# An even mixer in which the turned probabilities, not the scores, have two places in PSUM

## What is computed

```python
q, k, v, u, vv = split(z @ w_in)              # z: normed tokens; the context rows go through the same w_in
q, k = rms_norm(q) , rms_norm(k)              # per head, then rope on the 512 tokens
s = q @ k.T * dh ** -0.5                      # keys: a window of 1 to 3 blocks of 128, and the 256 context tokens
p = softmax(concat([s, sink]))[..., :-1]      # 8 heads, 6 query tiles of 128: 48 units
a = p @ v
u, vv = gelu(u), gelu(vv)
b = u * (ws @ rms_norm(vv) + bias)            # mixing inside chunks of 128 tokens, 8 groups
y = concat([a, b]) @ w_out
```

## Time and profile before

| | us |
|---|---|
| median of three runs | 3274.41 (3272.14 to 3275.29) |
| the profiled execution | 3274.63 |
| its span, first to last instruction | 3272.8 |
| PE busy | 3183.9 (97%) |
| DVE busy | 2219.2 (68%) |
| ACT busy | 1233.5 (38%) |

### The profile page before, as it was taken

The page is one execution under the profiler, slowest core; times in us unless marked ns, Lnnn a source line. Parts: engine busy times, 40 slices in busy tenths (PEclk is TensorE's granted clock), DMA queues, the critical chain, the costliest instruction groups (busy, mean ns, idle before and its releaser), DMA issues.

```text
span 3272.8 us, 50687 instructions
## 1 busy us (share of the span) xinstructions
PE 3183.9 (97%) x20376; PEld 2930.7 (90%) x20376; DVE 2219.2 (68%) x3792; ACT 1233.5 (38%) x2091; POOL 86.4 (3%) x189
## 2 busy tenths in 40 slices
PE   8999999998999999989999999989999999999999
PEld 6999999988899999989999999878888878788877
DVE  4979896466587777777777777675333666566754
ACT  4111112357553343354433343563222432334432
POOL 0000000001100000010000001000000000000100
PEclk9999999999999999999999999999999999999999
DMA  5545553210222222231222222112223321122232
GB/s 223 187 168 188 176 182 129 86 34 27 53 85 67 90 77 92 84 94 59 78 84 92 102 65 97 54 49 96 98 91 102 125 84 34 62 82 71 73 103 97
DMA packets 95321, 314.17 MB, mean 96 GB/s; under 512 B 11424, under 2 KB 15712, under 8 KB 93552
## 3 DMA queue, kind: packets, MB, share of 16 engines
q1 hardware_dynamic: 88128, 290.04, 26.4%
q0 software_dynamic: 6960, 20.88, 2.3%
HBM read 300.39 MB, written 4.19 MB: 93 GB/s over the span
## 4 chain that ended last, share of the span: by engine, by line
PE 48%; DVE 4%; ACT 2%; issue 1%; DMA 0%; ACTq 0%; DVEq 0%; SPq 0%
PE psum L690 32%; PE psum L1167 9%; DVE rawl L669 1%; PE psum L2842 1%; PE psum L1904 1%; DVE h L774 1%; PE psum L1887 1%; ACT wh L659 0%; PE psum L2865 0%; PE psum L2851 0%; PE psum L1728 0%; PE psum L3771 0%; DMA raw<-in_wdn 0%; PE psum L3289 0%; PE psum L1895 0%
## 5 line engine op out<-in xcount | busy, mean ns | idle before, releaser
L690 PE MATMUL psum<-zh,wh 128*128 128x512 f32 (+4 forms) x2352 | 756.6, 367 | 17.0 <-DVE ev L752 7.5
L659 ACT ACTIVATE wh<-raw 128x512 fp32r<-128x512 f32 (+3 forms) x551 | 447.3, 818 | 862.0 <-PE psum L690 471.5
L690 PE MATMUL psum<-zh,rawl 128*128 128x512 f32 (+4 forms) x2352 | 735.6, 358 | 0.0
L690 PE MATMUL psum<-zl,wh 128*128 128x512 f32 (+4 forms) x2340 | 732.2, 358 | 0.0
L669 DVE TENSOR_TENSOR rawl<-raw,wh 128x512 fp32r<-128x512 f32 (+3 forms) x551 | 502.6, 927 | 241.7 <-ACT wh L659 240.5
L690 PEld LDWEIGHTS psum<-zh,wh 128*128 128x128 f32 x2352 | 430.3, 189 | 69.3 <-issue 26.5
L1167 PE MATMUL psum<-formq,wh 128*128 128x386 f32 x1848 | 479.4, 341 | 10.2 <-DVE formq L971 3.5
L690 PEld LDWEIGHTS psum<-zh,rawl 128*128 128x128 f32 x2352 | 433.2, 189 | 41.2
L690 PEld LDWEIGHTS psum<-zl,wh 128*128 128x128 f32 x2340 | 431.0, 189 | 39.6 <-issue 2.9
L1167 PEld LDWEIGHTS psum<-formq,wh 128*128 128x128 f32 x1848 | 337.6, 189 | 15.3 <-DVE rawl L669 4.8
L774 DVE SCALAR_TENSOR_TENSOR h<-psum,mod,h 128x512 f32<-128x512 f32 (+1 forms) x288 | 169.9, 627 | 185.8 <-PE psum L690 185.6
(11 more groups left out here) (497 smaller groups left out, 4534.5 us busy)
## 6 DMA issues: line engine op xcount, KB each, us to landing
raw<-in_wup SPq DMA_DIRECT2D x176, 512.0 KB, 4.1
modw<-in_mod_w SPq DMA_DIRECT2D x128, 512.0 KB, 3.6
raw<-in_w_sw SPq DMA_DIRECT2D x36, 512.0 KB, 3.5
raw<-in_wdn SPq DMA_DIRECT2D x64, 256.0 KB, 3.7
raw<-in_wdn SPq DMA_DIRECT2D x32, 448.0 KB, 3.4
adaw<-in_ada_w SPq DMA_DIRECT2D x8, 1024.0 KB, 16.1
raw<-in_wdn SPq DMA_DIRECT2D x16, 512.0 KB, 3.9
raw<-in_od_in SPq DMA_DIRECT2D x16, 512.0 KB, 3.4
```

The lines of the kernel that those rows point to most:

```text
L659: nc.scalar.activation(hi_of(n, i), x, ACT.Copy).then_inc(w_hi, 1)
L690: last = nc.tensor.matmul(psum[:, at + to:at + to + e - s], w[:, q * P:(q + 1) * P], x[:, q, s:e], start=(q == 0 and j == 0), stop=(q == s ...
```

## The change

- From unit 32 on the turned probabilities have two places in turn (`turned_at`: E_PT, or column 0 for even units), and the scores keep their one. So every score now waits for the maximum of the unit just before, and the transposes from unit 33 on wait for the copy of the second unit before. Unit 32's transposes wait for the last uv drain, which its scores did before.
- From turn 33 on PE does the transposes ahead of the values.
- Mixing steps 0 to 5 go to turns 24 to 29, steps 6 to 11 to turns 34, 36, 38, 39, 41 and 43. `mb`, the buffer of the mixing on DVE, moves to a place of its own beside `ev_pt`, since in turns 24 to 29 the gate's buffer, whose place it shared, is in use.
- On DVE the drain of a uv tile comes right behind the maximum, ahead of division, inverse and all that follows. The lower keys of the second group go to turn 2. GELU of gate row 0 and the square behind it go from the last turn ahead of the units to turn 0.
- The order of the finished rows' split changes with the mixing.

```diff
-        mb = sb("mb", R_AT + words(2, T), [2, P])
+        mb = sb("mb", SCR_AT + words(4, 640), [2, P])
...
-                self.own_s = 1024 if u < SECOND_S or u % 2 else 0
+                self.turned_at = E_PT if u < SECOND_S or u % 2 else 0
...
-                return psum[:, self.own_s + c:self.own_s + c + w]
+                return psum[:, E_S + c:E_S + c + w]
...
-        DRAIN, CUBE, TANH, GELU = at(-3, 0), at(-2, 1), at(-2, 2), at(-1, 3)
-        VV_SQUARE, VV_GAIN, VV_SUM = [{i: k for i, k in x.items() if k < 4} for x in (at(-1, 3), at(0, 4), at(1, 5))]
+        DRAIN, CUBE, TANH, GELU = at(-3, 0), at(-2, 1), at(-2, 2), at(0, 3)
+        VV_SQUARE, VV_GAIN, VV_SUM = [{i: k for i, k in x.items() if k < 4} for x in (at(0, 3), at(0, 4), at(1, 5))]
...
-        MIX_STEPS = {34 + s: s for s in range(12)}
-        CAT_ROWS = [QROW, QROW + 1, QROW + 2, UROW, UROW + 1, UROW + 2, UROW + 3, QROW + 3]
-        CAT_CHUNKS = [4, 5, 6, 0, 1, 2, 3, 7]
-        CAT_STEPS = {31: 0, 33: 1, 39: 2, 42: 3, 44: 4, 47: 5, 48: 6}
+        MIX_STEPS = {24 + s: s for s in range(6)} | {34: 6, 36: 7, 38: 8, 39: 9, 41: 10, 43: 11}
+        CAT_ROWS = [QROW, QROW + 1, UROW, UROW + 1, QROW + 2, UROW + 2, UROW + 3, QROW + 3]
+        CAT_CHUNKS = [4, 5, 0, 1, 6, 2, 3, 7]
+        CAT_STEPS = {31: 0, 33: 1, 35: 2, 37: 3, 40: 4, 45: 5, 47: 6}
...
-                if i == SECOND_S:
-                    pe.wait_ge(drained, all_drained(EU))
-                elif i:
-                    pe.wait_ge(scores_read, i if i < SECOND_S else i - 1)
+                if i:
+                    pe.wait_ge(scores_read, i)
...
-                if i >= 1:
-                    pe.wait_ge(at_pc, i)
+                if i == SECOND_S:
+                    pe.wait_ge(drained, all_drained(EU))
+                elif i >= 1:
+                    pe.wait_ge(at_pc, i if i < SECOND_S else i - 1)
                 for j in range(len(u.vals)):
-                    last = nc.tensor.transpose(psum[:, E_PT + j * P:E_PT + (j + 1) * P],
+                    last = nc.tensor.transpose(psum[:, u.turned_at + j * P:u.turned_at + (j + 1) * P],
...
                 if i in VV_STEPS:
                     vv_rows_pe(pe, VV_STEPS[i])
+                if i in MIX_STEPS:
+                    mix_pe(pe, MIX_STEPS[i])
...
+                if i <= NE:
+                    transposes(i - 1)
                 if i % 2:
                     values(i - 3)
-                if i <= NE:
-                    transposes(i - 1)
...
+            def drain_beside(i):
+
+                if i in DRAIN:
+                    drain_row(dve, EU, EU.n[DRAIN[i]], ev[:, VVROW + DRAIN[i]])
...
+                drain_beside(turn - EV_TURNS)
                 beside_dve(dve, run, turn - EV_TURNS, 3)
-                if turn >= 3:
-                    g = turn - 3
-                    dve.wait_ge(ek_hi, EK_HI + g + 1)
-                    nc.vector.tensor_tensor(kl[:, g, :], ev[:, KROW + g, :], kh[:, g, :], ALU.subtract).then_inc(ek_lo, 1)
+                if turn == 3:
+                    keys_lower(0)
...
                 if 1 <= i < NE:
                     maximum(i)
+                drain_beside(i)
+                if i == 2:
+                    keys_lower(1)
```

More of the change, by code:

```diff
@@ L2210, in beside_dve @@
             row = lambda k: ev[:, VVROW + k, :]
-            if i in DRAIN:
-                k = DRAIN[i]
-                drain_row(dve, EU, EU.n[k], ev[:, VVROW + k])
             if i in GELU:
@@ L2441, in even_act @@
                         act.wait_ge(at_pv, (i - 1) // 2 * 2)
-                    nc.scalar.activation(ev_pt[:, u.u % 2, 0:u.w], psum[:, E_PT:E_PT + u.w], ACT.Copy).then_inc(at_pc, 1)
+                    nc.scalar.activation(ev_pt[:, u.u % 2, 0:u.w], psum[:, u.turned_at:u.turned_at + u.w],
+                                         ACT.Copy).then_inc(at_pc, 1)
                 if i >= 3 and i % 2:
@@ L2478, in maximum, with keys_lower @@
                                         ALU.mult, ALU.min).then_inc(at_s, 1)
+            def keys_lower(g):
+                dve.wait_ge(ek_hi, EK_HI + g + 1)
+                nc.vector.tensor_tensor(kl[:, g, :], ev[:, KROW + g, :], kh[:, g, :], ALU.subtract).then_inc(ek_lo, 1)
+            def drain_beside(i):
+                if i in DRAIN:
+                    drain_row(dve, EU, EU.n[DRAIN[i]], ev[:, VVROW + DRAIN[i]])
             run = Along(EU)
```

## The result

The changed kernel takes **3286.74 us** (median of five runs, 3285.95 to 3289.67). The kernel before, run beside it, takes 3275.18 (3272.14 to 3275.7). The ratio is 1.0039, with a 95% interval of 1.0029 to 1.0050: slower, by 0.4%. The forecast of +6.8 us had the direction and about half of the size. The measured time lies 0.7 us above the range.

A forecast was written before the change was run, and what follows sets the result against it. TensorE was taken as the bound nearly everywhere, with no hole until unit 30 and waits after. Terms -2.9 + 3.5 + 7.6 - 1.4 = +6.8 on 3274.63 gave 3281.4 us, range 3273 to 3286.

The forecast's parts named there:

- Term 1: Units 0 to 2: second uv tile's drain goes ahead, two short stalls, clock stays up; -2.9 us, bounds -4.3 and -1.3.
- the bound of one shorter spell (-1.3): Start, units 0 to 2: the clock falls once more, 3.2 us of work at half, 1.6 lost; sum -1.3 us.
- Term 2: Unit 20: PE waits 3.0 us for turned gate rows copied behind the drain, clock falls; +3.5 us, bounds +1.9 and +4.5.
- Term 3: Units 24 to 29: six mixing steps of 0.59 us plus waits at units 25, 26, 28; +7.6 us, bounds +6 and +9.
- Term 4: From unit 30: double turned probabilities, single scores, fewer mixing steps; lag 1.6, pairs -3.0; -1.4 us, bounds +1.6 and -7.9.
- The lag: Unit 30: last drain stands ahead of division, inverse and mixing, so unit 31's maximum and what follows come later; +1.6 us.
- The pairs: Five pairs of units, maximum of unit 36 to that of 46: 25.7 us in place of 28.73; -3.0 us.
- The end after unit 46 stays: Stretch behind unit 46's maximum: claimed to keep its length, no change.
- The tail did not pay back: Rival, tail: PE runs at its own work from unit 36, term 4 at -7.9; 3274.9 us, no change; chance 0.32.
- the 5.8 above which the prediction called itself wrong: Sign for the tail: pairs over 5.8 us, or under 4.6 us, would show the forecast wrong.
- Not all waits went: Faster rival, from unit 30: all PE waits go, term 4 at -16.4, sum -8.2; 3266.4 us; chance 0.06.
- The clock did not swing in units 20 to 29: Rival, units 20 to 29: stalls bring one longer low spell, 2.6 us more, sum +9.4; 3284.0 us; chance 0.12.

The follow-up runs named there:

- e7_late_division: Changed kernel with DVE dividing a pair's sums one turn later, behind the next maximum, from unit 34 on; 3285.98 us, ratio 1.0032.
- e5_square_early: Kernel before with only the second uv tile's drain ahead, lower keys at unit 2 and gate row 0's GELU product one turn earlier; 3270.27 us, ratio 0.9982.
- e1_drains_back: Changed kernel with the drains of units 1 and later back behind divisions, turned gate rows' copy and mixing's DVE part; 3280.43 us, ratio 1.0022.
- e9_mix_covered: Changed kernel with the first six mixing steps at odd units 23 to 33 in place of 24 to 29; 3283.99 us, ratio 1.0032.
- e4_places_back: Changed kernel with two places for scores and one for turned probabilities again, as before; 3282.31 us, ratio 1.0028.
- e3_values_first: Changed kernel with values ahead of transposes on PE again from unit 31 on; 3289.29 us, ratio 1.0051.
- e2_mix_back: Changed kernel with all twelve mixing steps in units 34 to 45 and the casts' order of before; 3278.72 us, ratio 1.0012.
- e6_order: Kernel of e5_square_early with transposes ahead of values from turn 33 on, two score places; 3268.51 us, ratio 0.9983.

## Why the prediction was wrong in size

- **Term 1: -2.9 forecast, -0.41 measured.** Both stalls came as worked out (1.3 and 1.4 forecast, 1.32 and 0.99 measured). The step that failed is "the nearest row is 803.5 to 807.4, idle 2.73 of 3.9 us, and there the clock stayed at 1.00. So I let it stay." The clock fell and stayed low over 6.8 us, also beyond the bound of one shorter spell (-1.3). In the forecast's own terms, -1.7 - 2.6 + 1.4 came out as -1.73 + 0.33 + 0.99: the 2.6 us of lower clock did not go. That the clock is the cause is shown from two sides: where nearly the same stalls did not bring it down (the execution of e7_late_division) the start was -2.75, close to the -2.9; and with one stall taken away (e5_square_early) the spell was 3.4 us long and the start -2.54. The one row in which it had held was not evidence enough, since it was one execution. And another row of the same trace spoke against it. The low spell at 847.4, which the earlier trace rows has, came behind three waits of PE that were all shorter than 1.3 us:

```profile
844.10 0.66 PE L2363 MATMUL psum<-ev_pt,vdup 128*64 128x128 f32 x8 [0.88 <-ACT ev_pt L2442]
...
846.16 0.41 PE L2350 MATMUL psum<-ident,ev_s 128*128 128x128 f32 x2 [0.82 <-ACT ev_pt L2442]
847.33 1.12 PE L2363 MATMUL psum<-ev_pt,vdup 128*64 128x128 f32 x8 [0.76 <-ACT ev_pt L2442]
```

- **Term 2: +3.5 forecast, +3.36 measured.** Right in place, in mechanism (the copy of the turned gate rows behind the drain) and in the choice that the clock falls. e1_drains_back takes it back whole. Its lower bound, +1.9 with no fall, is close to what e7_late_division's execution shows (+1.74).
- **Term 3: +7.6 forecast, +8.45 measured.** The waits came at the three units named, 1.59, 1.15 and 1.04 us (1.5, 1.3 and 1.3 forecast). The term mis-sized is the step itself: 0.59 was taken from mixing row to score row, but 8.45 less the three waits, 3.78, leaves 0.78 for each of the six, and the four steps without waits of e9_mix_covered cost 0.72. The clock stayed at 1.00 in these units, as forecast.
- **Term 4: -1.4 forecast, +1.8 measured** (+1.14, -0.93, +1.58). The lag was forecast at 1.6, and 1.14 came. The pairs were to gain 3.0 and gained 0.93. The step that failed is "the values, moved behind the transposes, fill PE while DVE and ACT work", beside which "2.57 a unit, 5.14 a pair" was worked out: that chain leaves out what hangs on the values. The sums' copy follows them, DVE's division waits for the copy, and the next maximum is queued behind the division. With the division out of that place (e7_late_division) the five pairs take 25.80 us. That this is near the forecast's 25.7 is in part luck: the pair of five-tile units 40 and 41, for which 5.14 was worked out, takes 6.14 us there and 6.13 in the changed kernel (6.23 before), and shorter units make up for it. With two score places the same waits of DVE cost the score nothing (e4_places_back). "The end after unit 46 stays" failed for two reasons that act together: the last maximum now comes behind a wait of 1.11 us for the sums' copy and behind `cat_lo` (L2285), and the end is 1.58 longer. Order of time on DVE:

```profile
856.18 0.29 DVE L2523 TENSOR_TENSOR ev<-ev,psum 128x128 f32<-128x128 f32 x1 [1.11 <-ACT ev L2446]
...
856.93 1.03 DVE L2285 TENSOR_TENSOR zl<-ev,zh 128x512 fp32r<-128x512 f32 x2
857.87 0.42 DVE L2474 CUSTOM_DVE_ANT_0 ev_s<-psum,ev_mask 128x256 f32<-128x256 f32 x1
```

With values first the end is 0.27 longer (e3_values_first). With the values behind, but the turns of mixing and casts as before, it is 0.45 shorter (e2_mix_back) and 0.25 shorter (e6_order); the clock fell later there, worth 0.7 and 0.5 us by an estimate from the last values and sums, so at one clock it would be some 0.2 longer. So the new turns of the mixing and the casts have a part in the 1.58; the prediction put the casts' new order at nothing.
- **The rivals.** The tail did not pay back: pairs of 5.56 us on average are near the 5.8 above which the prediction called itself wrong (the pair of units 40 and 41 alone is beyond it), and far from PE's own work. Not all waits went. The clock did not swing in units 20 to 29 beyond the fall after unit 20 that term 2 had. Its time, 3284.0, was the nearest of the four by luck: the time was lost elsewhere. The rule of the Trainium skill that stood behind it ("TensorE: Matmul & The Clock Gate", section "A second HAM failure mode: psum-queue depth-cycling") tells of frequent short idles that make the clock swing. The traces show nothing of it in units 24 to 29, with idles of 1.0 to 1.6 us, but it agrees with units 31 to 36 in six executions of other kernels (e1 to e4, e7 and e9, with 3.4 to 6.8 us at the lower level), e2_mix_back's with two low spells.

Terms 1 and 4 missed by 2.5 and 3.2 us and term 3 by 0.85, which with -0.14 of term 2 is the step from 6.8 to 13.19.

Two things stay open: why the clock falls behind a stall in one execution and not in the next, and what the drain at unit 30 costs by itself. The figures by stage are of one execution each, so a stage with a low spell in one kernel and none in the other (units 31 to 36 above all) can differ by up to 3.4 us (half of the longest spell) for that alone.

## What to carry to other kernels

When an instruction is moved on one engine, follow what hangs on its result through the queues of the other engines: here values behind transposes made a copy late, the copy held a division, and the division held the maximum that set the pace. Work that waits belongs where the engine waits anyway; six mixing steps cost 8.45 us among products and 1.4, low spells included, in the tail with one place for scores. Where a second buffer is to be given, look which of the two waits is the longer chain: the scores' place was worth 2.8 us more over five pairs than that of the turned probabilities.

## What the runs showed of the hardware that was not expected

A single stall of PE of 1.32 us, with two pauses of about 0.27 us ahead of it, brought the granted clock from 1.00 to 0.50 (2.4 to 1.2 GHz), in ten of the eleven executions here that had it. In that one a stall of 3.02 us at unit 20 left it at 1.00 too, and the same stall was followed by the lower clock in the changed kernel, e2_mix_back, e3_values_first, e4_places_back and e9_mix_covered. The same code thus has two outcomes, 4 us apart over both places. The low spell at the start lasted 3.4 us where the one stall stood alone and 6.8 where a second followed. From the maximum of unit 36 to that of 46, five scores of the changed kernel that waited 1.56 to 1.60 us each left the clock at 1.00, while in the kernel before it fell behind waits of 0.88, 0.82 and 0.76 us. So the length of a stall did not decide it alone.
